# Expert layer: small and large experts interleaved block by block, hidden activations turned one block later

## What is computed

```
gates = sum(one_hot(top_i, 8) * softmax(top_v), axis=-2)
for e in range(8):
    ye = (silu(xn @ w_gate[e]) * (xn @ w_up[e])) @ w_down[e]     # 1024 x 3584, 3584 x 1024
    out = out + gates[..., e:e + 1] * ye
```

## Time and profile before

| | us |
|---|---|
| median of 3 runs (1367.66 to 1368.17) | 1368.06 |
| the profiled execution | 1368.13 |
| its span in the trace | 1366.4 |
| expert layer, from the first `silu` at 386.4 to the copy of the last result at 1330.2 | 943.8 |

### The profile page before, as it was taken

The page is one execution under the profiler, slowest core; times in us unless marked ns, Lnnn a source line. Parts: engine busy times, 40 slices in busy tenths (PEclk is TensorE's granted clock), DMA queues, the critical chain, the costliest instruction groups (busy, mean ns, idle before and its releaser), DMA issues.

```text
span 1366.4 us, 17261 instructions
## 1 busy us (share of the span) xinstructions
PE 1325.6 (97%) x6404; PEld 1082.8 (79%) x6404; DVE 1154.0 (84%) x970; ACT 951.8 (70%) x874; POOL 71.5 (5%) x110
## 2 busy tenths in 40 slices
PE   8999999999999999999999999999999999999998
PEld 7776888888877887777777777888888888888887
DVE  6897655556889989999999999998898899889886
ACT  5676544446777777777777777777777777776775
POOL 2120910000200000000000000000000000000000
PEclk9999999999999999999999999999999999999999
DMA  8743765555299889999999999999999999999980
GB/s 305 266 130 89 256 203 195 185 185 162 86 357 347 317 323 359 393 395 393 394 393 390 380 394 395 394 372 371 337 351 375 377 349 359 376 337 359 358 329 31
DMA packets 197860, 422.46 MB, mean 309 GB/s; under 512 B 13064, under 2 KB 37392, under 8 KB 197776
## 3 DMA queue, kind: packets, MB, share of 16 engines
q1 hardware_dynamic: 197776, 421.35, 85.2%
HBM read 420.27 MB, written 1.05 MB: 308 GB/s over the span
## 4 chain that ended last, share of the span: by engine, by line
PE 74%; DVE 16%; ACT 5%; issue 3%; SPq 1%; DMA 1%; POOL 0%; ACTq 0%; DVEq 0%; POOLq 0%
PE ps L334 19%; PE ps L336 19%; PE ps L335 19%; DVE w_lo L314 12%; PE ps L885 5%; ACT w_hi L297 4%; PE ps L883 3%; PE ps L1048 1%; PE ps L865 1%; PE ps L1023 1%; PE ps L1049 1%; PE ps L862 1%; PE ps L882 1%; DMA raw<-in_attn_w_qkv_dram 1%; PE ps L1042 1%
## 5 line engine op out<-in xcount | busy, mean ns | idle before, releaser
L314 DVE TENSOR_TENSOR w_lo<-raw,w_hi 128x2048 fp32r<-128x2048 f32 x382 | 867.8, 2290 | 128.6 <-ACT w_hi L297 127.4
L297 ACT ACTIVATE w_hi<-raw 128x2048 fp32r<-128x2048 f32 x385 | 732.6, 1914 | 122.2 <-PE ps L336 100.0
L334 PE MATMUL ps<-w_hi,xe 128*128 128x512 f32 x448 | 178.4, 398 | 3.0 <-DVE w_lo L314 2.9
L336 PE MATMUL ps<-w_hi,xe 128*128 128x512 f32 x448 | 174.8, 390 | 0.0
L335 PE MATMUL ps<-w_lo,xe 128*128 128x512 f32 x448 | 174.5, 390 | 0.0
L334 PE MATMUL ps<-w_hi,h_t_hi 128*128 128x512 f32 x360 | 141.4, 393 | 0.5 <-DVE w_lo L314 0.5
L336 PE MATMUL ps<-w_hi,h_t_lo 128*128 128x512 f32 x360 | 140.3, 390 | 0.0
L335 PE MATMUL ps<-w_lo,h_t_hi 128*128 128x512 f32 x360 | 140.2, 389 | 0.0
L334 PE MATMUL ps<-w_hi,xb 128*128 128x512 f32 x280 | 111.4, 398 | 1.9 <-DVE w_lo L314 1.9
L885 PE MATMUL ps<-a_all,w_hi 128*128 128x512 f32 x308 | 109.8, 396 | 0.0
L336 PE MATMUL ps<-w_hi,xb 128*128 128x512 f32 x280 | 109.2, 390 | 0.0
(11 more groups left out here) (319 smaller groups left out, 1856.9 us busy)
## 6 DMA issues: line engine op xcount, KB each, us to landing
raw<-in_moe_w_gate_dram SPq DMA_DIRECT2D x112, 1024.0 KB, 7.6
raw<-in_moe_w_up_dram SPq DMA_DIRECT2D x111, 1024.0 KB, 7.4
raw<-in_moe_w_down_dram SPq DMA_DIRECT2D x111, 1024.0 KB, 7.4
raw<-in_attn_w_qkv_dram SPq DMA_DIRECT2D x11, 1024.0 KB, 12.6
raw<-in_ffn_w_gate_dram SPq DMA_DIRECT2D x11, 1024.0 KB, 5.3
raw<-in_ffn_w_up_dram SPq DMA_DIRECT2D x11, 1024.0 KB, 5.3
raw<-in_ffn_w_down_dram SPq DMA_DIRECT2D x11, 1024.0 KB, 5.0
raw<-in_ple_w_gate_dram SPq DMA_DIRECT2D x8, 1024.0 KB, 6.9
```

The source lines that it names most:

```text
L297: nc.scalar.activation(w_hi[:, u % SPLIT, :], raw_slot(u), ACT.Copy).then_inc(hi_ready, 1)
L314: nc.vector.tensor_tensor(w_lo[:, u % SPLIT, :], raw_slot(u), w_hi[:, u % SPLIT, :].bitcast(F32), ALU.subtract).then_inc(lo_ready, 1)
L334: nc.tensor.matmul(out, x[0], w[0], start=first, stop=False)
L336: return nc.tensor.matmul(out, x[1], w[0], start=False, stop=last)
```

## The change

After turn 0 the experts go in three pairs and a last one: small and large (rank 5 and 1), small and large (6 and 2), small and large (7 and 3), then large (4). In a pair the blocks alternate: block 0 of the small expert, block 0 of the large, block 1 of the small, block 1 of the large, and so on. The units are loaded in that order. All 334 units, all their matmuls and the slots of the two rings stay as they are, and so do the three small experts and their 64 slots.

With it goes the order inside a block. The hidden activations of a block are transposed in the following block, behind its second gate unit, and used by the down units of the block after that; a small expert's go into `p_t_hi`, a large one's into `h_t_hi` and `h_t_lo`, since both are live. ScalarE splits unit 4 before it copies the hidden part and forms `silu`. VectorE multiplies (`hiddens`) behind the split of unit 6. The two experts of a pair accumulate in PSUM banks 6, 7 and 3, 4. Gathers are spread as four pieces over banks 5 and 2, scatters one by one behind single units (tables `SCATTERS`, `LAST_SCATTERS`), and ScalarE copies the transposed picks. The sort makes 20 places per token tile where there were 8, because a fallback for crowded experts needs 12 more; the fallback runs only if an expert has more tokens than slots.

```diff
-RANK_AT = (0, 5, 6, 7, 1, 2, 3, 4)
-FEW_AT = (1, 2, 3)
+ROOM = (SLOTS, FEW, SLOTS, FEW, SLOTS, FEW, SLOTS, SLOTS)
...
+RANK_AT = (0, 5, 1, 6, 2, 7, 3, 4)
+PLACES = NE + len(SECOND)
...
+        PAIR_BLOCKS = [(f, e) for f in range(FB) for e in range(2)]
...
+            def pair(k, first=False):
+
+                for f, e in PAIR_BLOCKS:
+                    few, x, g = e == 0, (xe, xb)[e], block_at_seq(f, e)
...
+                            gate_or_up(u + 2 * n + half, n, half, x, g, k, few)
+                            if n == 0 and half == 1:
...
+                                transpose_hidden(g - 1, k, few=e == 1)
...
+                    f_down, g_down = (f - 1) % FB, g - 2
+                    t_down = e + 1 if f else e - 1
+                    down(u + 4, f_down, 0, g_down, t_down, k, few=few)
...
+                    down(u + 5, f_down, 1, g_down, t_down, k, few=few)
...
+            def pair(k, first=False):
+
+                for f, e in PAIR_BLOCKS:
+                    g, u = block_at_seq(f, e), pair_unit(f, e, first)
+                    for n in range(4 if first and f == 0 and e == 0 else 6):
+                        split_hi(u + n + AHEAD, k)
...
+                        if n == 2:
+                            hidden_hi(g - 1, k, few=e == 1)
+                            silus(g, u + 1, k)
...
+            def pair(k, slots, first=False):
...
+                        if n == 2:
+                            hidden_lo(g - 1, k, few=e == 1)
+                        if n == (3 if bare else 4):
+                            hiddens(g, u + 3, k)
...
-            turn(1, 0, few=True)
-            turn(2, 0, few=True)
-            turn(1, 2, few=True)
-            turn(2, 2)
+            pair(0, first=True)
+            pair(2)
             with act.Fori(3, pairs + 1) as it:
-                turn(1, (it - 1) * 2)
-                turn(2, (it - 1) * 2)
-            turn(1, turns - 1, end=True)
+                pair((it - 1) * 2)
+            last_turn(turns - 1)
```

More of the change, by code:

```diff
@@ L1049, in product_few, with down @@
                 return nc.tensor.matmul(out, x, w[1], start=False, stop=last)
-            def down(u, f, half, g, k=0, end=False, h_t=(h_t_hi, h_t_lo), few=False):
+            def down(u, f, half, g, t, k=0, end=False, h_t=(h_t_hi, h_t_lo), few=False):
                 unit(u, k)
@@ L1066, in down, with gate_or_up @@
                 last.then_inc(unit_used, 1)
[L1068 to L1073, removed]
+            def gate_or_up(u, n, half, x, g, k=0, few=False):
+                unit(u, k)
+                if half == 0:
+                    pe.wait_ge((silu_ready, hidden_ready)[n], g + FB * k)
+                for c in range(4):
+                    d, w = 4 * half + c, weights(u, c, 0, 512, 512)
+                    if few and n == 1:
+                        both = x[:, 2 * d * P + FEW:2 * d * P + FEW + P]
+                        last = product_few(ps[:, n, :], both, w, d == 0, d == KD - 1)
+                    else:
+                        rows = x[:, 2 * d * P:(2 * d + 1) * P], x[:, (2 * d + 1) * P:(2 * d + 2) * P]
+                        last = product(ps[:, n, :], rows, w, d == 0, d == KD - 1)
+                last.then_inc(unit_used, 1)
@@ L1075, in turn, with transpose_picks, first_turn @@
+            def transpose_picks(k, experts):
+                pe.wait_ge(added, 4 + 4 * k)
+                for e in range(experts):
+                    for tt in range(TT):
+                        at = (e * TT + tt) * P
+                        last = nc.tensor.transpose(ps[:, 5, at:at + P], pick_of(e, tt).bitcast(F32), ident[:, :])
+                last.then_inc(pick_transposed, experts)
+            def first_turn():
                 for f in range(FB):
-                    u, g = turn_unit(t0, f), JF + FB * t0 + f
@@ L1077, in turn @@
-                    for n, freed in ((0, silu_ready), (1, hidden_ready)):
+                    u, g = turn_unit(0, f), JF + f
+                    gather = f == FB - 1
+                    for n in range(2):
                         for half in range(2):
[L1079 to L1094, removed]
@@ L1095, in turn @@
[L1095 to L1097 removed]
+                            if f == 0 and n == 0:
+                                pe.wait_ge(xe_lo_ready, half + 1)
+                            gate_or_up(u + 2 * n + half, n, half, xe, g)
+                            if gather and n:
+                                gather_piece(half, 0, g)
+                        if f == 1 and n == 0:
+                            transpose_hidden(g - 1)
@@ L1115, in turn @@
[L1115 to L1119, removed]
+                    if f:
+                        down(u + 4, f - 1, 0, g - 1, 0)
+                        if gather:
+                            gather_piece(2, 0, g)
+                            gather_piece(3, 0, g)
+                        down(u + 5, f - 1, 1, g - 1, 0)
+                        if not gather:
+                            transpose_hidden(g)
@@ L1130, in _ @@
-            turn(1, 2, few=True, few_before=True)
-            turn(2, 2, few_before=True)
+            pairs = pe.value_load(more[0:1, 1:2], min_val=0, max_val=EXTRA_TURNS // 2) + 3
+            pair(0, first=True)
+            pair(2)
             with pe.Fori(3, pairs + 1) as it:
-                turn(1, (it - 1) * 2)
-                turn(2, (it - 1) * 2)
-            turn(1, turns - 1, end=True)
+                pair((it - 1) * 2)
+            last_turn(turns - 1)
             for half in range(2):
-                down(U_TURN + half, FB - 1, half, JF + FB - 1, turns, end=half == 1, h_t=(a_hi, a_lo))
+                down(U_TURN + half, FB - 1, half, JF + FB - 1, 1, turns, end=half == 1, h_t=(a_hi, a_lo))
@@ L2203, in _ @@
-            turn(0, few_next=(True, True))
+                    u, g = turn_unit(0, f), JF + f
+                    for n in range(0 if f else 1, 4):
+                        split_lo(u + n + AHEAD)
+                        if f == 1 and n == 1:
+                            hidden_lo(g - 1)
+                        if f == 1 and n == 3:
+                            sort_experts()
+                        if f == 2 and n == 2:
+                            place_experts()
+                        if f in (3, 4) and n == 2:
+                            rows_lo_of(f - 3)
@@ L2212, in _ @@
+            pair(0, iota_few[:, :], first=True)
+            pair(2, iota_few[:, :])
             with dve.Fori(3, pairs + 1) as it:
-                turn(1, (it - 1) * 2)
-                turn(2, (it - 1) * 2)
-            turn(1, turns - 1, end=True)
+                pair((it - 1) * 2, iota_next)
+            last_turn(turns - 1)
             split_lo(U_TURN + AHEAD, turns)
```

528 lines of the change are left out of this document (336 added, 192 removed).

## The result

The changed kernel takes 1372.75 us (median of 7 runs, 1370.93 to 1374.84), the one before 1368.08 (7 runs). The ratio is 1.0031, with a 95% interval of 1.0021 to 1.0041: slower by 4.7 us, 0.3%. Forecast were 1374.6 us and +6.5. The profiled execution took 1371.23 us, 3.1 more than that of before.

What follows compares the result with a forecast made beforehand. It took small blocks to be bound by the chain from a freed slot through ScalarE and VectorE to TensorE, with three slots. Terms +4.2 + 0 + 1.3 + 1.0 = +6.5 us on 1368.13 gave 1374.6 us, range 1358 to 1386.

Steps and rivals of the forecast that it cites:

- The bound: Small blocks: TensorE waits 1.90 us on the chain from a freed slot through ScalarE and VectorE, with three slots.
- Part 1: A small and a large block: 32.56 us against 32.36, +0.2 us each, x 21 = +4.2 us.
- Part 2: Gathers, scatters and result splits: costed at nothing, with -3 and +6 us as ends.
- VectorE stays behind: Rival: result splits, adds and picks in VectorE's gapless stretch delay following blocks, 0.6 us more a couple, 1387 us; chance 0.10.
- Part 3: Sort and placing in turn 0: longer operations there are not covered, +1.3 us, between 0 and 2.
- Part 4: Counters in registers: silu 0.14 us later in looped turns, in 7 small blocks, +1.0 us, between 0 and 3.
- The sum: Whole kernel: +4.2 + 0 + 1.3 + 1.0 = +6.5 us on 1368.13, giving 1374.6 us.
- Balance wins: Rival: ScalarE and VectorE gain lead in the large block, waits fall to half or none, 1350 down to 1331 us; chance 0.20.
- the low part of unit 5: Small block of a couple: walked as ready at 13.0 us; the balance rival decides if it is ready before 12.0.
- The rule of the Trainium skill on interleaving regimes: Interleaving may help where the most-contended engine changes between regimes; by it the sum would be -40 us, not +4.2.
- the same section's remark on consistent bubbles: A repeated gap on an engine that should be full can mean too few buffers; by it the waits stay.
- The fallback: Rival: an expert with more tokens than slots adds ten turns of some 110 us; given no chance.

Runs made afterwards that it cites:

- order alone: Kernel before, with ScalarE rounding unit 4 before it forms silu in turns 1 to 7: 1363.97 us, ratio 0.9960.
- halved loads: Kernel before, with only half of each expert unit loaded from turn 1 on, all other work kept: 1368.15 us, ratio 0.9997.
- the fourth slot: Changed kernel with a fourth slot for split units from turn 1 on: 1341.01 us, ratio to the kernel before 0.9799.
- the later order: Changed kernel with four slots and hidden copy, silu and hidden split one unit later, behind unit 5: 1335.50 us, ratio to the kernel before 0.9752.
- the later product alone: Changed kernel, three slots, with only VectorE's product of gate and up behind unit 7 in place of unit 6: median 1371.91 us.

## Why the prediction was right

**The bound.** That the small block waits on the chain and not on VectorE's load or the loads from HBM was right for the kernel before: order alone brought the wait from 1.46 to 1.03 us, halved loads brought nothing.

**Part 1, the couple.** Forecast 32.56 us and four waits of 2.36 in all; measured 32.44 to 32.57 in plain couples, with 2.55 in the one shown. The excess over 32.36 is 0.12 a couple, 2.5 us in place of 4.2. The reason given, that three slots do not carry the large block's spare time over, is shown by the fourth slot: -31.7 us in the changed kernel.

**Part 2** was costed at nothing. By the trace it is what remains of the 1.65 us behind turn 0: 1.65 - 2.5 = -0.9 us. One couple in each pair takes 32.8 to 32.9 us: in the first pair two `pick` operations stand on VectorE in its gapless run there (642.09), and TensorE's third wait is 0.89 in place of 0.51. So in such a couple *VectorE stays behind* came true, and other places more than made up for it.

**Part 3, sort.** Forecast 1.3 us, measured 2.1 without it and 1.9 in the blocks concerned. Mis-sized: the placing went from 1.58 us (421.23 to 422.81) to 2.96 (421.64 to 424.60), of which the new last two operations over 128 numbers, with their 0.3 us each, were the part taken too low; and the copy of the picks, credited with 0.3, gave nothing where TensorE waits. Turn 0 as a whole grew by 1.6.

**Part 4, registers.** Forecast 1.0 us, measured none: a looped couple takes 32.44 us, one written out 32.48. This is the term that was wrong and not only too large. The 0.14 us of `silu` seen before lay in time that nothing waited for, and it hardly appears on the roundings that now stand in front (idle 0.80 and 0.82 us, against 0.80 and 0.87 written out). What the loop does show is the wait put down to issue, in the place of one for `w_lo`; the waits of the looped couple come to 2.33 us in place of 2.55.

**The sum.** By the two profiled executions, both at a mean granted clock of 1.000, +3.1 us against +6.5: 2.5 for the couples, -0.9 for part 2, 1.6 for turn 0, less 0.1. The medians differ by 4.7. Two of the changed kernel's seven runs have a mean clock of 1.000 and take 1370.93 and 1371.23; the five at 0.997 to 0.999 take 1372.57 to 1374.84. Of the kernel before, six of seven lie between 1367.66 and 1368.26 and one at 1369.67. So some 1.5 us of the median's 4.7 go with the clock and belong to no step of the prediction, and that the median came within 2 us of the forecast is in part luck: without them the sum is twice what was measured, by part 4 (+1.0, measured none), by an excess per couple taken too high (+4.2, measured 2.5) and by part 2 (0, measured -0.9). Whether the change itself makes the slower clock more frequent is open.

**The rivals.** *Balance wins* was wrong for three slots and right for four: the low part of unit 5, named as the point from which it decides, comes 0.26 us late with the fourth slot and in time with the later order. The rule of the Trainium skill on interleaving regimes (Perfetto Trace Analysis, Optimization Strategy) holds here on the condition that the same section's remark on consistent bubbles names: enough buffers. What the prediction did not see is that interleaving is worth more than TensorE's and VectorE's balance: it also averages the loads. With `silu` behind unit 4 and four slots, the kernel that keeps the small experts together stops at 1364 on 394 GB/s and the interleaved one reaches 1341, or 1335 with the later order; with halved loads the first comes to 1348 and the last to 1333. *VectorE stays behind* at 0.6 us in every couple did not happen. The fallback did not run.

## What to carry to other kernels

Averaging two regimes needs a place to store the average: before interleaving, walk one period through the buffers and see how far ahead the helpers can get, since busy shares cannot say it. An order and a buffer can each be worth little alone and much together, so a null result of one is no verdict on it. When a wait is removed in a stage that streams, compare its bytes over its new time with the highest rate seen: here the small turns used 393 GB/s of the 394 that the loads gave, and the first wait that was shortened met them.

## What the runs showed of the hardware

Loads of 1 MB from HBM by one core levelled off at 394 GB/s (395 at most over 50 us) in every stretch that asked for more, with a share of the 16 engines of 1.04, and went to 203 GB/s, all that was asked for, when halved. The Trainium skill (DMA: Bandwidth & Descriptors, Specifications) has 358 GB/s as the limit from HBM for a core and 435 for the fabric. That page of the Trainium skill says, beside its measured rates, that about 358 is what each gets when both cores of a pair stream. This kernel ran on one core, and its 394 lies between the two; no run here puts a second core to work.

The granted clock is not the same in every execution of one kernel, and where it falls can be read. In the trace of the kernel with the later product alone (1373.35 us, mean 0.997):
```profile
412.00:416.00 4.00, 4.00 (x12) 3.16 (x11) 4.00 (x3) 0.19 (x2) 0.00 (x0) 0.59 0.94 314
544.00:548.00 4.00, 3.17 (x8) 2.50 (x9) 4.00 (x3) 1.80 (x2) 0.00 (x0) 0.62 0.92 320
```
The third number from the end is the granted clock; inside both stretches it stands at 0.50, the level of 1.2 GHz. Both begin just behind a wait of TensorE for `w_lo`, of 1.78 and 2.23 us. The changed kernel's profile has the same waits, 1.78 and 2.25 us, and holds 1.00 behind them. The blocks concerned take 20.67 and 16.82 us in the one and 19.07 and 15.27 in the other. So each fall cost some 1.6 us here, and why the same wait brings it in one execution and not in another no run shows. A difference of 2 or 3 us in this kernel is not to be read from single executions whose clocks differ.
